# The end of the gated layers: two branch pieces turned ahead of the last gate job, the pieces ahead of the weight rounding and the table load, the first two output jobs in K halves

## The reference

```python
def gla_mixer(h, s0, w_in, w_a2, b_a, g_on, w_out):
    B, L, _ = h.shape
    q, k, v, g, a = _split(h @ w_in, [GLA_KEY_DIM, GLA_KEY_DIM, GLA_VAL_DIM, GLA_VAL_DIM, GLA_GATE_RANK])
    ...
    o, s = gla_recurrence(heads(q, GLA_DK) * (GLA_DK ** -0.5), heads(k, GLA_DK),
                          heads(v, GLA_DV), heads(logf, GLA_DK), s0)
    o = rmsnorm(o, g_on).astype(h.dtype).reshape(B, L, GLA_VAL_DIM)
    return (o * jax.nn.silu(g)) @ w_out, s
```

## Time and profile before

| | us |
|---|---|
| median of 3 runs (1245.56 to 1248.56) | 1247.09 |
| the profiled execution | 1254.17 |
| its span | 1252.4 |
| PE busy in it | 1179.7 (94%) |
| VectorE, ScalarE, GpSimd busy | 591.7, 568.4, 377.7 |
| mean granted TensorE clock | 0.975 |

### The profile page before, as it was taken

How to read it: one execution, slowest core, us unless ns; L and a number is a source line. 1 busy time by engine, 2 the same in 40 slices (tenths; PEclk the granted TensorE clock), 3 DMA queues, 4 the chain that set the end, 5 groups by cost and what they waited for, 6 DMA issues and landing times. The chain is left out here.

```text
span 1252.4 us, 25047 instructions
## 1 busy us (share of the span) xinstructions
PE 1179.7 (94%) x9935; PEld 1041.8 (83%) x9935; DVE 591.7 (47%) x1179; ACT 568.4 (45%) x1100; POOL 377.7 (30%) x322
## 2 busy tenths in 40 slices
PE   6999999799999999999979999999999999999797
PEld 5789887799668998889964459999999879978596
DVE  4362344655259999100024544479265262244532
ACT  6442367543432354545554344322453343366643
POOL 4445231144223321122200013533444245312230
PEclk8999999899999999999989999999999999999898
DMA  5334235123414356676778974222321125333301
GB/s 148 102 102 152 85 102 169 54 73 100 134 47 137 102 169 203 220 236 213 221 258 324 353 270 118 73 84 81 119 74 37 64 71 186 102 119 102 118 2 72
DMA packets 132909, 168.78 MB, mean 135 GB/s; under 512 B 25545, under 2 KB 98601, under 8 KB 132784
## 3 DMA queue, kind: packets, MB, share of 16 engines
q1 hardware_dynamic: 120729, 152.59, 37.7%
q10 hardware_dynamic: 12062, 14.59, 3.3%
HBM read 150.70 MB, written 16.81 MB: 134 GB/s over the span
## 5 line engine op out<-in xcount | busy, mean ns | idle before, releaser
L664 POOL TENSOR_TENSOR w_lo<-raw,w_hi 128x512 fp32r<-128x512 f32 (+2 forms) x267 | 355.8, 1363 | 778.0 <-ACT w_hi L1341 778.0
L700 PE MATMUL psum<-h_hi,w_hi 128*128 128x272 f32 x1616 | 474.9, 294 | 21.3 <-DVE h_lo L2170 15.7
L702 PE MATMUL psum<-h_hi,w_lo 128*128 128x272 f32 x1616 | 470.1, 291 | 0.0
L701 PE MATMUL psum<-h_lo,w_hi 128*128 128x272 f32 x1616 | 467.8, 290 | 0.0
L700 PEld LDWEIGHTS psum<-h_hi,w_hi 128*128 128x128 f32 x1616 | 306.3, 190 | 33.9 <-issue 27.8
L701 PEld LDWEIGHTS psum<-h_lo,w_hi 128*128 128x128 f32 x1616 | 306.9, 190 | 0.0
L702 PEld LDWEIGHTS psum<-h_hi,w_lo 128*128 128x128 f32 x1616 | 306.0, 189 | 0.0
L1341 ACT ACTIVATE w_hi<-raw 128x1024 fp32r<-128x1024 f32 (+1 forms) x137 | 135.0, 1034 | 122.3 <-PE psum L702 91.1
L700 PE MATMUL psum<-w_hi,h_hi 128*128 128x512 f32 (+2 forms) x352 | 126.1, 358 | 0.4 <-ACT idx_relu L1623 0.4
L701 PE MATMUL psum<-w_lo,h_hi 128*128 128x512 f32 (+2 forms) x352 | 123.0, 350 | 0.0
L702 PE MATMUL psum<-w_hi,h_lo 128*128 128x512 f32 (+2 forms) x352 | 122.5, 348 | 0.0
(11 more groups left out here) (309 smaller groups left out, 1476.1 us busy)
## 6 DMA issues: line engine op xcount, KB each, us to landing
raw<-in_cache_k_dram SPq DMA_DIRECT2D x128, 256.0 KB, 3.1
raw<-in_gla_w_in_dram SPq DMA_DIRECT2D x23, 1024.0 KB, 5.5
spare<-in_cache_v_dram SPq DMA_DIRECT2D x36, 512.0 KB, 5.6
raw<-in_dsa_w_in_dram SPq DMA_DIRECT2D x17, 1024.0 KB, 6.0
raw<-in_cache_v_dram SPq DMA_DIRECT2D x28, 512.0 KB, 5.4
gla_s_in<-in_state_gla_dram SPq DMA_DIRECT2D x16, 512.0 KB, 7.9
raw<-in_gla_w_out_dram SPq DMA_DIRECT2D x8, 1024.0 KB, 6.7
out_dram<-gla_s_in ACTq DMA_DIRECT2D x16, 512.0 KB, 4.4
```

What stands on the lines that cost most here:

```text
L664: pool.tensor_tensor(copies(key, pair_view(w_lo, key)[:, k]), raw_copies(key, k), copies(key, pair_view(w_hi, key)[:, k].bitcast(F32)), AL ...
L700: pe.matmul(out, lh, rh, start=start, stop=False)
L701: pe.matmul(out, lh, rl, start=False, stop=False)
L702: return pe.matmul(out, ll, rh, start=False, stop=stop)
```

## The change

- `blocks`: after a GLA layer the first eight of the 16 output jobs are now (m 0 to 3, part 0) and then (m 0 to 3, part 1); before it was three and three.
- PE: `out_transposes` of pieces 0 and 1 stands before gate job 15 and those of pieces 2 to 5 behind it; their banks are written out (4, 5, then 3, 4, 5, 6).
- PE: the first two output jobs are one function, `first_two`: k = 0 to 3 of job 0, k = 0 to 3 of job 1, k = 4 to 7 of job 0, k = 4 to 7 of job 1. `last_rows` is called in the middle of the third job (at k = 4), not behind the second.
- ScalarE: h_hi of pieces 0 and 1 come right behind the squares of tile 3, then SiLU of gate block 7, h_hi of pieces 2 and 3, the first half of the rounding of out 1, h_hi of pieces 4 and 5, the second half, the table load, the square sums, Ln and Exp, and `sequence(7)` behind those.
- VectorE: pieces 0 and 1 (both steps) come ahead of gate part 15, the copy of the sample rows behind piece 5.

The weights, the sizes and the count of matmuls stay as they are.

The diff, cut to its core (left out: the new stream of `piece` and `low` calls in VectorE's `gla`, which the rows above show, and context):

```diff
             if L == 0:
                 return [(4 * mh + m, part) for mh in range(2) for part in range(2) for m in range(4)]
-            first = {0: [(0, 0), (1, 0), (2, 0), (0, 1), (1, 1), (2, 1)], 1: [(0, 0), (1, 0), (0, 1), (1, 1)],
+            first = {0: [(m, part) for part in range(2) for m in range(4)], 1: [(0, 0), (1, 0), (0, 1), (1, 1)],
                      2: []}[KINDS[L - 1]]
             return first + [x for x in ((m, part) for m in range(KT) for part in range(2)) if x not in first]
...
                         if x % 2:
                             mm.then_inc(*sig("yT", t, x // 2))
+                def first_two():
+
+                    key = (L, "out", 0)
+                    wh, wl = pair_view(w_hi, key), pair_view(w_lo, key)
+                    c = PARTS[0][1]
+                    hi, lo = H[L % 2]
+                    bs = [claim(m, ("proj", (L, "out", m), 0), ("resid", (L, "out", m), 0)) for m in range(2)]
+                    for k0 in (0, KT // 2):
+                        for m in range(2):
+                            for k in range(k0, k0 + KT // 2):
+                                if m == 0:
+                                    split_in(key, k)
+                                    ready(k, 0)
+                                mm = product(psum[:, bs[m], 0:HC], wh[:, k, m * P:(m + 1) * P], wl[:, k, m * P:(m + 1) * P],
+                                             hi[:, k, c], lo[:, k, c], k == 0, k == KT - 1)
+                            if k0:
+                                mm.then_inc(*sig("proj", (L, "out", m), 0))
+
                 order = blocks(L + 1)
                 used = [m // 2 for m, _ in order]
                 for i, (m, part) in enumerate(order):
                     x, key = m // 2, (L, "out", m // 2)
                     wh, wl = pair_view(w_hi, key), pair_view(w_lo, key)
                     done = x not in used[i + 1:]
-
-                    def first(k, part, x=x, key=key, new=used.index(x) == i, ask=m == 0 or KINDS[L] == 2 and x == 0):
+                    if between and i < 2:
+                        if i == 0:
+                            first_two()
+                        continue
+
+                    def first(k, part, x=x, key=key, new=used.index(x) == i, ask=m == 0 or KINDS[L] == 2 and x == 0,
+                              rows_now=between and i == 2):
+                        if rows_now and k == KT // 2:
+                            between()
                         if new:
                             split_in(key, k)
                         if ask:
                             ready(k, part)
                     y = m % 2
-                    part_job((L, "out", m), P, "resid", (next_bank(range(3) if last or between and i < 2 else range(NBANK)),),
+                    part_job((L, "out", m), P, "resid", ({2: 2, 3: 6}[i] if between and i < 4 else next_bank(range(3) if last else range(NBANK)),),
                              lambda k: (wh[:, k, y * P:(y + 1) * P], wl[:, k, y * P:(y + 1) * P]), h_pair(L), KT,
                              ((("item", key),),) if done else (), None,
                              first, (PARTS[part],))
-                    if between and i == 1:
-                        between()
                     if last and x and done:
                         turn_blocks(x - 1)
                 if last:
...
             def out_transposes(L, t, half):
                 pe.wait_ge(*on("o_norm", L, t))
-                b = claim(next_bank(range(3, NBANK)), ("oT", L, t, half), ("oT_read", L, t, half))
+                b = {(0, 0): 4, (1, 0): 5, (2, 0): 3, (0, 1): 4, (1, 1): 5, (2, 1): 6, (3, 0): 3, (3, 1): 4, (SMP, 1): 5}[t, half]
+                claim(b, ("oT", L, t, half), ("oT_read", L, t, half))
                 if t == SMP:
                     for x in range(2):
                         mm = pe.transpose(psum[:, b, x * P:(x + 1) * P], v_s[:, x * P:(x + 1) * P], ident[:])
...
                         gate_job(4 * t + 4)
                         attend(t + 1)
                     sequence(2 * t + 1)
+                    if t == NP_T - 1:
+                        out_transposes(L, 0, 0)
+                        out_transposes(L, 1, 0)
                     gate_job(4 * t + 5 if t < NP_T - 1 else 15)
-                for half in range(2):
-                    for t in range(3):
-                        out_transposes(L, t, half)
+                for t, half in OUT_PIECES[2:6]:
+                    out_transposes(L, t, half)
                 def last_rows():
                     for half in range(2):
...
                 act.wait_ge(*on("rstd_ln", *key))
                 act.activation(y, ln, ACT.Exp, scale=-0.5).then_inc(*sig("rstd_y", *key))
-            def split_hi(n):
+            def split_hi(n, halves=(0, 1)):
                 key = weights[n]
                 act.wait_ge(*on(f"raw{slot[key]}", key))
...
                 if n >= 2:
                     act.wait_ge(*on("proj", ("item", weights[n - 2])))
                 kk = items[index[key]][2]
-                for half in range(2) if len(pieces(key)) > 1 else (0,):
+                for half in halves if len(pieces(key)) > 1 else (0,):
                     k = slice(half * kk // 2, (half + 1) * kk // 2) if len(pieces(key)) > 1 else slice(0, kk)
                     copy(copies(key, pair_view(w_hi, key)[:, k]), raw_copies(key, k)).then_inc(*sig("split_hi", key, half))
...
                     if t < NP_T - 1:
                         decay(2 * t + 3)
                         gate_block(2 * t + 1)
-                    sequence(2 * t + 1)
-                    if t < NP_T - 1:
+                        sequence(2 * t + 1)
                         root(slice(4 * t, 4 * t + 4), t)
                         gate_block(2 * t + 2)
-                gate_block(KT - 1)
+
+                def branch_hi(i):
+                    out_hi(L, *OUT_PIECES[i], tmp_og[:, i % 4])
+
+                branch_hi(0)
+                branch_hi(1)
+                gate(L, gate_g, KT - 1, ("gate_dve", (L, "g", KT - 1), 1))
+                branch_hi(2)
+                branch_hi(3)
+                split_hi(pair_of[(L, "out", 1)], (0,))
+                branch_hi(4)
+                branch_hi(5)
+                split_hi(pair_of[(L, "out", 1)], (1,))
                 act.preload_act_table_set(EXP_LN)
                 squares(SMP)
                 root(slice(12, 17), SMP)
+                sequence(DB - 1)
                 act.wait_ge(*on("s_now", L, NCH))
                 act.dma_start(gla_state_prompt[j, 0].rearrange("h k v -> k h v"),
                               s_now[:, 0, :].rearrange("p (h v) -> p h v", h=GH)).then_inc(*sig("stores_gla", L, n=16))
-                for i, (t, half) in enumerate(OUT_PIECES):
-                    out_hi(L, t, half, tmp_og[:, i % 4])
+                for i in range(6, len(OUT_PIECES)):
+                    branch_hi(i)
                 next_input(L + 1)
 
```

37 lines of the change are left out of this document (25 added, 12 removed).

## The result

The changed kernel takes 1238.8 us in the median of 10 executions (1236.4 to 1243.3), the kernel before 1247.4 in as many (1244.0 to 1256.5). The ratio is 0.9926, with a 95% interval of 0.9909 to 0.9942: by it the change makes the kernel 9.2 us faster, 7 to 11. (Ratios use the executions counted as fast alone, medians all of them.) The forecast was 1233.0, range 1229.5 to 1237.5. The sign was right, the size 5.8 us off, and the median lies outside the range. The profiled execution took 1239.08 (span 1237.3, mean granted clock 0.978).

What follows compares the result with a forecast made beforehand. PE, busy 94%, bounds the kernel; 19.5 us are lost at two layer ends, chiefly waiting for h_lo. Less 2 × 2.5 of waits and 0.2 + 0.2, the gain is 14.1: 1247.09 to 1233.0 us, range 1229.5 to 1237.5.

Steps and rivals of the forecast that it cites:

- Two pieces turned ahead: Eight transposes (0.93 us) before gate job 15, no work added; their h_lo end by 1174.9, ahead of gate part 15.
- Wait 1: PE's wait for h_lo of piece 2 before output job 0: 1.0 us, job starting about 1177.7 instead of 1184.29.
- Wait 2: PE's wait for h_lo of piece 5 after its first 24 matmuls, VectorE held up by GpSimd: 0.2 to 1.75 us.
- Wait 3: PE's wait for the norm of the last rows, in the middle of the third output job: 0 to 1.1 us.
- The clock at the place: At both layer ends the new waits are each shorter than 1.78 us, so PE keeps the full clock, 1.00.
- Rivals 1 and 5: 1: clock falls once a layer anyway, 1235 to 1237, chance 0.22. 5: clock stays low through output jobs, 1257, 0.02.
- rival 2: Every VectorE instruction with two SBUF inputs meets GpSimd: waits 2.85 us a layer, gain 13.0, time 1234.1; chance 0.15.
- 3.8 us of slow time: Slow-clock loss behind PE's idle waits at the ends of layers 0 and 3, counted as gain beside the 15.7 us.
- The bank wait of 0.2: Layer 0: PE's early pieces wait for VectorE's copy out of the last attention tile's banks; 0.2 us, none in layer 3.
- The 0.2 for job 8: Layer 0: out 2 is split one job later, so job 8 waits for its last quarter, 0 to 0.3, taken as 0.2.
- Sum, 14.1 us: Total gain at both layer ends: 19.5 − 2 × 2.5 − 0.2 − 0.2 = 14.1 us.
- Rival 3: Hand-overs of ScalarE, VectorE and PE each 0.3 to 0.5 us longer: gain 6 to 9, time 1238 to 1241; chance 0.10.

Runs made afterwards that it cites:

- the kernel with the late rounding: Changed kernel with both halves of the rounding of out 1 on ScalarE moved behind piece 5; 1238.4 us, ratio 0.9910.
- no early pieces: Changed kernel with no piece turned ahead of gate job 15, all six behind it; 1240.1 us, ratio 0.9917.
- whole jobs: Changed kernel with the first two output jobs run whole again, not in K halves; 1244.0 us, ratio 0.9951.
- the filler: Kernel before, with 58 added transposes into an unused bank ahead of the output jobs; 1253.1 us, ratio 1.0025.
- second pair of profiles: Both kernels run again without edits; before 1249.0 us, after 1237.6 us; profiled spans 1243.6 and 1233.4.
- index products mended: Both kernels with layer 1's index products over 128 rows instead of 64, the others zeros; before 1249.7 us, changed 1233.2 and again 1234.0.

## Why the prediction was right here and wrong there

**Bound and place: right.** PE's waits for h_lo were the price, and they are 4.6 us now: 11.1 us of the 14.1.

**Two pieces turned ahead: right.** h_lo of the first two was to end 4.1 us behind PE's end of sequence(7), and ended 3.96 behind; gate part 15 was to end 4.66 behind, and did 4.5.

**Wait 1, 1.0 us: measured 0.96**, in both layers and in every profile of the whole change.

**Wait 2, 0.2 to 1.75: measured 1.35 to 1.39**, and by the mechanism named: h_lo beside GpSimd's w_lo. The two took 1.6 us longer than two without it, one GpSimd operation of 1.48 (5.92 / 4). The Trainium skill, "SBUF — State Buffer", section "Who interferes with whom", says that VectorE's operations with two inputs in SBUF contend with GpSimd's reads, and that one of the two blocks until the other is done. By the trace the two h_lo took 1.22 and 1.76 us in place of 0.68, so both were held up, and moving GpSimd's work away took the delay with it. L2128 reads one tile only and still took 1.07 beside GpSimd in the kernel with the late rounding, against 0.16 without GpSimd (before) and 0.25 beside it in the changed kernel: not every meeting costs the same. The same section says that such an operation (a tensor_scalar) contends too when it runs in one of the modes with two port pairs; which mode it ran in, the trace does not show.

**Wait 3, 0 to 1.1: measured 0**, but with 0.2 us to spare: L2131 took 0.85 in place of 0.17 as feared, and the kernel with the late rounding has this wait at 2.6.

**The clock at the place: right**, 1.00 in both layers. Other runs show how near it was: it fell in one layer of two behind a gap of 2.32 (no early pieces) and of 2.85 (whole jobs), in both behind the 2.6 of the late rounding, in none behind 1.5 or less. Rivals 1 and 5 did not come. The mechanism of rival 2 did in part, both h_lo and L2131 being slowed, but with 2.3 us of waits a layer and not 2.85. The 3.8 us of slow time were real in the sum but wrongly described, as the filler shows: they were mostly the chain's, and went because the chain got shorter.

**Small terms.** The bank wait of 0.2 in layer 0 came in two of the three profiles of the change. The 0.2 for job 8 did not come.

**Sum, 14.1 us: measured 14.1** in the first pair of profiles and 14.7 in the second.

**The step that failed** is the one behind the sum: "nothing says that the place differs between runs, so I take it off both: 1240.1 profiled, median 1247.09 − 14.1 = 1233.0". The place does not differ. But the step takes for granted that the rest of the program stays as it is, and the rest was not the same: by the means only 10.8 us of the 14.1 to 14.7 arrived. The index products of layer 1 came at low clock in two of three profiles of the change and in neither of before, for 7.2 us in the first; in the second pair of profiles other short low stretches took the difference. That the first profile (1239.1) met the 1240.1 that was forecast for it is luck: three short low stretches of before, absent from it, made up for most of the index products. The base was off too: 1247.09 is the median of three runs, 104 executions have a mean of 1249.3, and "the runs differ by ±1.5 us" was read from those three where the 104 lie between 1244 and 1256.5. With the index products mended in both kernels the difference of the means is 1249.8 − 1233.3 = 16.5 us, some 15 to 18 by the scatter of twelve executions each. That is the local 14.1 to 14.7 and up to 3 us more, for which no cause is shown beyond fewer low stretches in those profiles. That the mended kernel stands at 1233.3 does not save the forecast, which was for the other.

The price of one such stretch could be read before: the profile of before had the clock as a column, and its low stretches were more than those at the two layer ends. Its own 7 us above the median said that such stretches come and go. That went into no term and no rival. Rival 3 names the measured time (1238 to 1241) and rival 1 comes near it (1236), but for reasons that did not occur: there was no fall at the place, and the hand-overs were no longer than counted. How low clock elsewhere depends on the change, if it does, stays open.

## What to carry to other kernels

A gain that is worked out at one place reaches the total only if the rest keeps its clock: list all low-clock stretches of the profile and what runs in them, and widen the range by one of them. Where products use only part of TensorE's rows, try filling the others with zeros: here it cost no matmul time, was worth 5 us in the changed kernel and nothing in the one before. Mixing such products into full work without that made both kernels slower. When a wait is set by an operation of GpSimd beside VectorE, look at what that operation will meet after the move before moving it.
